# Three expert pairs of the old block moved from before the first picks to behind them, in a DeepNorm decoder layer with PEER experts

## The reference, cut to what matters

```python
q = (xb @ w_query).reshape(L, PEER_HEADS, 2, PEER_QUERY_DIM // 2)
s = jnp.einsum('lhpd,hpkd->lhpk', q, sub_keys)
vals, idx = lax.top_k(s, K)
cand = (vals[..., 0, :, None] + vals[..., 1, None, :]).reshape(L, PEER_HEADS, K * K)
best, pos = lax.top_k(cand, K)
expert = jnp.take_along_axis(cidx, pos, axis=-1)
gate = jax.nn.softmax(best, axis=-1)
h = jax.nn.gelu(jnp.einsum('ld,lhkd->lhk', xb, expert_u[expert]), approximate=False)
out = jnp.einsum('lhk,lhkd->ld', h * gate, expert_v[expert])
```

## Time and profile before

| what | value |
|---|---|
| median of 3 runs | 3097.0 us (3091.28 to 3106.02) |
| the profiled execution | 3092.87 us, span 3091.0 us |
| PE, DVE, ACT, POOL busy | 76%, 72%, 36%, 39% of the span |
| DMA engines busy by gathers (q0) | 84.0% of the span |
| DMA engines busy by SP's loads (q1) | 12.7% of the span |
| moved | 1235.90 MB, mean 400 GB/s |
| chain that ended last | DVE 32%, PE 29%, DMA 25%, ACT 6% |

### The profile page before, as it was taken

How to read it: one execution, slowest core, us unless ns; L and a number is a source line. 1 busy time by engine, 2 the same in 40 slices (tenths; PEclk the granted TensorE clock), 3 DMA queues, 4 the chain that set the end, 5 groups by cost and what they waited for, 6 DMA issues and landing times.

```text
span 3091.0 us, 37872 instructions
## 1 busy us (share of the span) xinstructions
PE 2352.3 (76%) x11842; PEld 1330.6 (43%) x11842; DVE 2239.9 (72%) x5638; ACT 1121.6 (36%) x3530; POOL 1195.2 (39%) x1028
## 2 busy tenths in 40 slices
PE   8996878868788677877779778886778767785654
PEld 7773435424356343544346343542435434351111
DVE  5488656986679766897658966699657986678645
ACT  4123533254333533235322353224432363323222
POOL 0034452344423454234533345234443344434442
PEclk9998999989899898988989889988988889887777
DMA  8199999999999999999999999999999999999997
GB/s 350 42 383 412 420 421 406 412 413 420 420 408 418 417 420 420 397 407 419 420 419 404 416 420 421 407 399 413 420 420 404 418 418 420 420 372 421 410 421 323
DMA packets 189000, 1235.90 MB, mean 400 GB/s; under 512 B 21752, under 2 KB 21880, under 8 KB 54656
## 3 DMA queue, kind: packets, MB, share of 16 engines
q0 software_dynamic: 147456, 1073.81, 84.0%
q1 hardware_dynamic: 39168, 154.32, 12.7%
q10 hardware_dynamic: 2176, 5.36, 0.4%
HBM read 1229.21 MB, written 4.19 MB: 399 GB/s over the span
## 4 chain that ended last, share of the span: by engine, by line
DVE 32%; PE 29%; DMA 25%; ACT 6%; issue 5%; POOL 2%; DVEq 0%; POOLq 0%; SPq 0%; ACTq 0%
DMA ring<-in_uv,expert_used 24%; DVE ring L1849 14%; PE expert_sum L1007 13%; PE bank L614 7%; PE bank L621 2%; PE bank L603 2%; ACT diag L1336 2%; POOL ring L541 2%; DVE arena L1477 2%; DMA chunk<-in_weights 1%; DVE conv L1497 1%; DVE arena L1792 1%; DVE arena L1789 1%; DVE arena L1492 1%; DVE arena L1486 1%
## 5 line engine op out<-in xcount | busy, mean ns | idle before, releaser
L541 POOL DMA_INDIRECT ring<-in_uv,expert_used x1024 | 1195.0, 1167 | 1863.2 <-PE expert_sum L1007 1413.1
L1007 PE MATMUL expert_sum<-ring,diag 128*64 128x512 f32 x4096 | 1185.8, 708 | 639.1 <-ACT diag L1336 638.1
L1849 DVE CUSTOM_DVE_ANT_0 ring<-ring,x_pair 128x1024 f32<-128x1024 f32 x1024 | 1227.6, 1223 | 478.6 <-DMA ring<-in_uv,expert_used 472.8
L1007 PEld LDWEIGHTS expert_sum<-ring,diag 128*64 128x64 f32 x4096 | 312.3, 155 | 1261.0 <-issue 1246.4
L1329 ACT ACTIVATE h_raw<-h_raw 128x2 f32<-128x2 f32 x512 | 104.1, 203 | 1457.5 <-DVE h_raw L1849 1456.4
L1336 ACT ACTIVATE diag<-const,h_raw 128x64 f32<-128x64 f32 x1024 | 292.6, 332 | 4.9 <-PE expert_sum L1007 4.9
L1332 ACT ACTIVATE h_raw<-h_raw,gate_used 128x1 f32<-128x1 f32 x1024 | 245.6, 286 | 16.8
L614 PEld LDWEIGHTS bank<-oT,chunk 128*128 128x128 f32 x1344 | 152.7, 192 | 22.7 <-issue 22.7
L614 PE MATMUL bank<-oT,chunk 128*128 128x128 f32 x1344 | 158.6, 277 | 0.0
L1477 DVE MAX8 arena<-arena 128x8 f32<-128x128 f32 (+1 forms) x384 | 103.7, 325 | 32.6 <-ACT arena L1282 27.3
L603 PE MATMUL bank<-chunk,oT 128*128 128x256 f32 x464 | 110.0, 388 | 0.0
(11 more groups left out here) (276 smaller groups left out, 2621.6 us busy)
## 6 DMA issues: line engine op xcount, KB each, us to landing
chunk<-in_weights SPq DMA_DIRECT2D x228, 512.0 KB, 8.2
ring<-in_weights SPq DMA_DIRECT2D x17, 1024.0 KB, 23.9
ring<-in_uv,expert_used POOLq DMA_INDIRECT x1024, 15.5
chunk<-in_weights SPq DMA_DIRECT2D x4, 1024.0 KB, 20.4
x<-in_x SPq DMA_DIRECT2D x8, 512.0 KB, 14.6
out<-oT ACTq DMA_DIRECT2D x8, 512.0 KB, 9.2
o_cat<-in_xT SPq DMA_DIRECT2D x7, 512.0 KB, 14.6
xT_even<-in_xT SPq DMA_DIRECT2D x4, 512.0 KB, 10.0
```

Of the source, the lines that this page charges most:

```text
L541: pool.indirect_dma_start(out=place(n, j), out_offset=None, in_=io["uv"], in_offset=bass.IndirectOffsetOnAxis(ap=expert_used[:, j:j + 1], ...
L1007: mm = pe.matmul(expert_sum[i][c * SPAN:(c + 1) * SPAN, :], diag[:, (j % DIAGS) * SPAN:(j % DIAGS + 1) * SPAN], place(n, j)[:, D + i * 512 ...
L1849: dve.tensor_tensor_reduce(u, u, x_pair[:, (j % 2) * D:(j % 2 + 1) * D], 1.0, 0.0, ALU.mult, ALU.add, h_raw[:, j:j + 1]).then_inc(dotted.s ...
```

## The change

Four numbers in `EARLIER` are changed. Old pairs no longer stand at `qu0`, `more0` and `rest0`, and `pick0` has four. The sum of the table is the same, and no instruction is added or removed. On DVE, ACT and PE the pairs of these marks move together.

```diff
--- before.py
+++ after.py
@@ -147,7 +147,7 @@
     rope=1, gates=1, taps1=1, scores=2, taps2=1, softmax=2, turn_p=2, att_o=2,
     norms=1, decay=1, kk=1, aT=1, pow2=2, pow4=1, pow8=1, prod3=1, turn32=1, merge32=1, turn64=1,
     merge64=1, solve=2, ws0=1, kv0=2, ws1=1, kv1=1, dn=2, o_T=1, out0=1, out1=1, out2=1, out3=1,
-    scale1=1, shift1=1, x1_T=1, half_q=1, qu0=1, top0=1, more0=1, sel0=1, rest0=1, pick0=1,
+    scale1=1, shift1=1, x1_T=1, half_q=1, qu0=0, top0=1, more0=0, sel0=1, rest0=0, pick0=4,
 )
 NEXT_IN = ("more1", "sel1", "rest1", "pick1", "top2", "more2", "sel2", "rest2", "pick2", "top3", "more3")
 AFTER_IN = ("sel3", "rest3", "pick3")
```

## The result

The changed kernel took **3108.14 us** (median of 20 runs, 3103.06 to 3114.11) beside 3101.03 for the kernel before on the same chips (20 runs). The ratio is **1.0024, 95% interval 1.0016 to 1.0032**: 7 us slower, where 14 us faster was forecast. By the bound of 0.5% it is no change, but its sign is certain. The profiled execution has a span of 3105.0 us (3091.0 before).

The account below looks back on a forecast made before the run. The prediction took the DMA engines as the bound: 20.2 us won round the first picks less 5.6 given back behind the turn-over, say 14 us, brings the median from 3097.0 to 3083 us. Its range was 3071 to 3098, holding 0.8.

Parts of the forecast that it names:

- That is all that this change can win: Round each block's first picks: seven 20 us stretches lack 27.4 us of DMA work in all, the most to win.
- The picks, POOL and PE: Block 5: picks ready 10.7 us earlier, first new gather 4.2 us earlier, released by PE; 20.2 us won over seven blocks.
- The rule against it: Gathers in twos, by the skill's single-transfer rate, lose 2 us a block; gain 2 to 3 us, not 14.
- What is moved to later: Pair 64's gathers go out 8.5 us later, as PE adds pairs later; cost nothing, at most 2 us a block.
- SP's last query chunk: nothing, or up to 1.9 us: PE wants the last query chunk sooner behind its issue, by rest0's pair: costs nothing, or up to that pair's 1.9 us.
- The turn-over moves by 0.3: `read_sums` and all behind it on DVE, ACT and PE start 0.3 us later in block 5.
- What it gives back: Behind the turn-over ten gathers run out before the eleventh, a new hole: 5.6 us over seven blocks, bounds 0 and 10.
- All is kept: Rival, chance 0.17: the margin behind the turn-over holds, nothing is given back; 20 to 27 us faster, 3070 to 3077.
- thin refill: Rival, chance 0.16: gathers in twos leave the DMA engines short between them; 2 to 6 us faster, 3091 to 3095.
- Not the picks but PE: Rival, chance 0.15: PE's mark comes no earlier, so new gathers go out when they do now; 3094 to 3100 us.
- The slower one: Rival, chance 0.07: PE idles between `query_chunks(3)` and pair 64, its clock falls, own pairs come 7 us later; 3110 to 3123.
- Every instruction on an engine is cheap as long as they have work: Premise for the whole kernel: gathers fill 84.0% of the DMA engines' span, SP's loads 12.7%, so these engines are the bound.

Follow-up runs that it names:

- the late turn-over in before: Kernel before with three unused DVE instructions (some 2.6 us together) put ahead of `read_sums` in each of the seven turn-overs: ratio 1.0025 to before.
- rest0's pair with the turn-over kept: Kernel before with rest0's pair moved behind the picks on DVE and ACT alone, ACT's pair 63 ahead of `queries_out(3)`: ratio 1.0004 to before.
- the fourth run: Changed kernel with PE taking three pairs ahead of the last query chunks and ACT working pairs 61 to 63 ahead of `queries_out(3)`: ratio 1.0006 to before.
- rest0's pair alone: Kernel before with only the pair at rest0 moved behind the picks (rest0=0, pick0=2): ratio 1.0011 to before.
- the two runs with qu0 kept: Changed kernel with qu0=1 and pick0=3: ratio 1.0035 to before; the same with ACT's pairs 62 and 63 ahead of `queries_out(3)`: 1.0025.

## Why the prediction was wrong, point by point

*"That is all that this change can win".* Holds as a bound, but it was taken for what closing the hole is worth. Two pairs of kernels have the eleventh gather in nearly the same place and 17 us of hole between them: after and the late turn-over in before (0.2 us apart, 1.0024 and 1.0025), and rest0's pair with the turn-over kept and before (0.6 us apart, 1.0004, interval 0.9992 to 1.0015). Neither shows a gain. A gain of some 4 us is not ruled out by these intervals, one of 17 is.

*The picks, POOL and PE.* Right in mechanism and nearly in size: picks 11.7 us earlier for 10.7, the first new gather released by PE and 2.5 us earlier for 4.2. I had PE without a break; it waits for weights (1.14 and 0.56 us in block 5), and these 1.7 us are all that the 2.5 lack of 4.2. From PE's start of pair 60 to the gather it is 2.7 us, as forecast. The stretches round the picks lack 19.1 us less for 20.2.

*The rule against it* (gathers in twos on the queue). The new gathers' data is moved behind +36, past the end of the seven stretches above. From +20 to +50 blocks 1 to 6 run at 408 to 417 GB/s (30 us less the 0.3 to 0.9 us that lack in each). By the Trainium skill, "DMA: Bandwidth & Descriptors", section Measured, a single 1 MB transfer would have 78%. Here other transfers were queued beside them in these blocks, and the trace shows no such loss. In block 7 5.2 of these 30 us lack. I was right to take it lightly.

*"What is moved to later", taken as nothing.* Pair 64's gathers are 9.4 us later for 8.5, but its data is not "2 us behind the issue": the second gather, issued at 2009.32, lets DVE start at 2023.29, 14 us on. I had compared the time of the data with the end of what was queued, and left out that the gather stands behind all of it. That cost DVE two waits of 2.55 us but not the turn-over: PE came to pair 64 later still, 0.3 us behind its tiles in block 5. Taking nothing for this term came out right, for another reason than mine.

*"SP's last query chunk: nothing, or up to 1.9 us".* 10.0 us over seven blocks, 1.4 each, less than half of it at the last chunk itself. The bound was right and the value chosen wrong: PE without a break says that a load is not late, and not by how much it is early. In block 5 of before the last half chunk was issued at +17.1, landed at +28.5, 11.4 us on, and was wanted some 12.8 us behind its issue (an estimate: 4.6 us into the 7.41 us of PE's row at 2001.91): 1.4 us of slack. After, it was issued at +14.4 and wanted 10.9 us behind that, 1.9 sooner, and it took 11.5: the wait of 0.56. The other wait, 1.14 us at 1998.89, is of the same kind and was not in the forecast at all: a half chunk issued at -2.5 that lands at +11.4 in both kernels, with PE there sooner. The loads themselves are hardly slower; PE lost pairs whose work had covered them.

*"The turn-over moves by 0.3".* 1.7 us in block 5, 2.4 in the mean. In block 5 it is the two waits for weights, 1.7 us, by which PE was later at pair 60 than forecast. The rest of that sum held: first diagonals 3.3 us behind PE's mark (3.34 measured, ACT's copy and table load in it), pair 64 then 10.1 us behind the mark (9.7 measured). In the mean pair 64 starts 1.9 us later than before, and the order on PE and ACT gives back 1.4 of the 2.4 us (the fourth run). The two blocks with 4.6 us are not explained; their `read_sums` starts 3.9 and 3.6 us behind the start of pair 64 on PE, where it is 2.1 elsewhere, and the profile names no releaser within the kernel.

***"What it gives back", 5.6 us: the term that failed, 29.5 measured.*** The working followed ten gathers to the eleventh, found 3.3 us of margin, and stopped there. But the eleventh to the sixteenth go out from +56.9 to +71.3 before, and the seventeenth at +75.5: six gathers, 6 x 2.5 = 15 us of work, for 18.6 us; the full rate of the earlier trace rows's last line lives, for as long as DVE has no break, on what the hole had left over. The margin was not one of 3.3 us that decides: whatever is filled ahead of the turn-over is missing behind it, nearly us for us, where the eleventh gather is in nearly the same place (17.2 us closed and 14.0 opened between the late turn-over and after, 16.7 and 16.4 between before and rest0's pair with the turn-over kept). The bound of 10 for this term came from drains of 2 us, which measure how fast an engine runs empty and not how long it is fed too little.

*The rivals.* "All is kept" and "thin refill" did not happen. "Not the picks but PE" had its condition in part, query chunks that PE waits for, which took 1.7 of the 5.7 us; the new gathers came earlier all the same. The slower one (0.07) has the right place, the turn-over, and the wrong mechanism: the three pairs took 5.37 us, 1.8 each, at the granted clock of 1.00 of the stretch 2004 to 2024 (2.4 GHz), with no fall to 1.2 GHz; and its price rested on a margin that wasn't there. Its chance was too low because I held the turn-over to be late only if the clock fell.

*"Every instruction on an engine is cheap as long as they have work"*, from the share of 84.0% and 12.7%. That is the root. In block 5 the DMA engines are the bound for some 200 of the 368 us only. In the other stretch the rate is high too (396 to 419 GB/s), as the ring's reserve feeds it, but DVE sets the pace. The forecast asked where the DMA engines lack work; it had to ask as well whether DVE has any idle time left with which to use data that comes sooner.

## What to carry to other kernels

Where two engines are nearly full in turn, a hole of the one is only worth filling if the consumer has idle time behind it before the producer's buffer is full again: read the consumer's busy time from the hole to where it next waits for data, not the producer's share over the span. With a bounded ring, follow the supply past the first refill until the rates meet, for a gap closed in front of the consumer's busy stretch comes out at its end. And work taken away in front of a load's first use takes the load's slack away: an engine without a break shows that its loads are in time, not by how much, so read issue and landing before giving the move no price.

## What the runs showed of the hardware that I had not expected

The time of a weight load hardly depended on the hole. The last half chunk of query weights (0.5 MB) took 11.3 to 11.9 us from issue to landing in the seven blocks of before, 10.8 to 12.1 in after and 11.4 to 12.2 with rest0's pair alone, though PE waited for weights 0.0, 10.0 and 5.7 us. Only where new gathers were out at +22 to +23 (the two runs with qu0 kept) did it take longer, 12.9 to 13.2 us; it was issued 2 us earlier there too, and no run tells the two apart.

A gather of 1 MB on busy queues took long whatever the kernel: pair 64's two in block 5 landed 18.7 and 21.9 us behind their issue in before, and the second took 14 us from issue to use in after. The first gather of block 7 in before, issued on the empty queues at 2746.54, landed after 5.9 us.
